# Twenty-two instead of sixteen expert tiles scored ahead of the expert loop of a two-block transformer kernel

## What is computed

```python
def peer(x, w_q, sub_keys, u_tab, v_tab):
    q = (xt @ w_q).reshape(T, PEER_HEADS, 2, PEER_HALF)
    s = jnp.einsum('thpd,hpkd->thpk', q, sub_keys)
    s_top, i_top = lax.top_k(s, PEER_TOPK)
    cand = s_top[:, :, 0, :, None] + s_top[:, :, 1, None, :]
    best, pos = lax.top_k(cand, PEER_TOPK)
    gate = jax.nn.softmax(best, axis=-1)
    act = gelu(einsum('td,thkd->thk', xt, u_tab[eid]))
    return einsum('thk,thkd->td', gate * act, v_tab[eid])
```

## Time and profile before

| | |
|---|---|
| Median of three runs | 3553.58 us (3553.43 to 3553.96) |
| The profiled execution, its own time | 3553.21 us |
| Its span | 3551.4 us |
| Mean granted TensorE clock | 0.966 of full speed |
| Busy share: PE, PEld, DVE, ACT, POOL | 94%, 82%, 66%, 42%, 11% |
| First L696 of the three layers | at 256.01, 1369.77 and 2744.74 us |
| Moved by transfers | 511.71 MB, 144 GB/s on average |

### The profile page before, as it was taken

The page is one execution under the profiler, slowest core; times in us unless marked ns, Lnnn a source line. Parts: engine busy times, 40 slices in busy tenths (PEclk is TensorE's granted clock), DMA queues, the critical chain, the costliest instruction groups (busy, mean ns, idle before and its releaser), DMA issues. The chain is left out here.

```text
span 3551.4 us, 58703 instructions
## 1 busy us (share of the span) xinstructions
PE 3327.6 (94%) x20974; PEld 2901.9 (82%) x20974; DVE 2329.5 (66%) x4413; ACT 1485.1 (42%) x2257; POOL 387.8 (11%) x412
## 2 busy tenths in 40 slices
PE   7889999999987798999999996989889999999998
PEld 5788899999986587899999996578478889999996
DVE  4697666666656588766666665555459766666665
ACT  3336444444444325544444433333333644444444
POOL 0156000000000047300000000000015700000000
PEclk9899999999998699999999998999999999999999
DMA  5420555555543131355555545100232055555553
GB/s 208 152 74 28 188 184 186 189 189 185 183 164 150 52 139 48 105 193 184 187 189 189 185 164 185 63 1 1 95 147 79 22 187 189 189 183 185 187 189 145
DMA packets 127130, 511.71 MB, mean 144 GB/s; under 512 B 14624, under 2 KB 15520, under 8 KB 119712
## 3 DMA queue, kind: packets, MB, share of 16 engines
q1 hardware_dynamic: 127008, 510.09, 40.4%
HBM read 508.99 MB, written 1.05 MB: 144 GB/s over the span
## 5 line engine op out<-in xcount | busy, mean ns | idle before, releaser
L610 PE MATMUL ps<-xh,uhigh 128*128 128x256 f32 x3072 | 870.4, 283 | 0.0
L612 PE MATMUL ps<-xh,ulow 128*128 128x256 f32 x3072 | 869.3, 283 | 0.0
L611 PE MATMUL ps<-xl,uhigh 128*128 128x256 f32 x3072 | 869.2, 283 | 0.0
L610 PEld LDWEIGHTS ps<-xh,uhigh 128*128 128x128 f32 x3072 | 588.3, 191 | 14.6 <-issue 1.4
L611 PEld LDWEIGHTS ps<-xl,uhigh 128*128 128x128 f32 x3072 | 588.3, 192 | 14.3 <-issue 1.4
L612 PEld LDWEIGHTS ps<-xh,ulow 128*128 128x128 f32 x3072 | 588.3, 191 | 0.0
L760 ACT CAST uhigh<-stream 128x1024 fp32r<-128x1024 f32 x336 | 352.8, 1050 | 442.4 <-DMA stream<-in_u 442.4
L992 DVE TENSOR_TENSOR ulow<-stream,uhigh 128x1024 fp32r<-128x1024 f32 x330 | 404.4, 1225 | 194.5 <-ACT uhigh L760 194.4
L997 DVE TENSOR_TENSOR stream<-stream,big 128x256 f32<-128x256 f32 x336 | 217.9, 649 | 411.2 <-ACT stream L822 411.1
L628 PE MATMUL ps<-vhigh,chigh 128*128 128x512 f32 x1536 | 479.8, 394 | 1.5 <-DVE vlow L1008 1.5
L628 PE MATMUL ps<-vlow,chigh 128*128 128x512 f32 x1536 | 476.0, 391 | 0.0
(11 more groups left out here) (498 smaller groups left out, 4383.6 us busy)
## 6 DMA issues: line engine op xcount, KB each, us to landing
stream<-in_u SPq DMA_DIRECT2D x369, 512.0 KB, 4.2
stream<-in_v SPq DMA_DIRECT2D x369, 512.0 KB, 3.5
big<-in_wq SPq DMA_DIRECT2D x24, 1152.0 KB, 7.1
stream<-in_ab_w_in SPq DMA_DIRECT2D x4, 2048.0 KB, 10.9
stream<-in_c_w_qf SPq DMA_DIRECT2D x16, 512.0 KB, 3.5
stream<-in_c_w_ig SPq DMA_DIRECT2D x4, 2048.0 KB, 9.0
big<-in_w_gates SPq DMA_DIRECT2D x4, 2048.0 KB, 8.3
spare<-in_u SPq DMA_DIRECT2D x15, 512.0 KB, 3.6
```

Of the source, the lines that this page charges most:

```text
L610: pe.matmul(out, high[:, cols], c.xh[:, k, :], start=k == 0, stop=False)
L611: pe.matmul(out, high[:, cols], c.xl[:, k, :], start=False, stop=False)
L612: ins = pe.matmul(out, low[:, cols], c.xh[:, k, :], start=False, stop=k == KD - 1)
```

## The change

One constant is raised:

```diff
-HELD = 16
+HELD = 22
 SLOTS = 4
 WCOLS = 2 * KD * P + 2 * P
 GROUP = 2
```

## The result

The changed kernel takes 3559.02 us in the median (3553.26 to 3563.12, 22 runs) against 3553.85 us (3551.72 to 3556.03, 22 runs) before: a ratio of 1.0016, interval 1.0010 to 1.0022. That is 5.2 us slower. The profiled execution took 3557.37 us, its span 3555.2.

The account below looks back on a forecast made before the run. PE, 94% busy, bounds the kernel except in an idle stretch ended by a chain from POOL's last low part. 3 x (0.2 + 1.6) = 5.3 us on 3553.2 gives 3558.5, median 0.4 higher: 3559 us, range 3550 to 3566.

Parts of the forecast that it names:

- PE's work is moved and not saved: Per layer: loop 33.7 us less, held outputs 16.6 and held scores 17.3 more, so PE's work grows by 0.2 us.
- The stretch moves with POOL's last low part: PE's idle stretch before the first L696 is pushed on by 17.28 us per layer, not filled.
- the chain: Transfer, ACT, POOL, DVE: 15.25 us from the last held low part's end to the first L696, moving with the held tiles.
- The turns: POOL's low parts alternate with DVE's L925 and L869, 3.33 us a turn; the chain starts 1.6 us late per layer.
- Gate matrix and loads at nothing: Wider gate_held and ACT's shorter copies: 0, bounds -1.8 and +1.4 us; v loads slowing the u tile: 0, at most 0.9 per layer.
- the first (the idle time is filled): Rival: PE's three waits of about 5.41 us before the distances are all covered; 3538 us; chance 0.05.
- The second: Rival: the stretch shifts but DVE's four instructions fit POOL's gaps or the delay is made good; 3554 us; chance 0.18.
- the fourth: Rival: L945 gets its turn between POOL's two low parts, 2.3 us back per layer; 3552 us; chance 0.08.
- The third: Rival: DVE and POOL instructions exclude each other at full length, 3.62 us a turn; 3562.5 us; chance 0.21.
- the rule of the Trainium skill: The shared pair of ports is held for the full instruction and the other side fully blocks; by it, 3562.5 us.
- the signs named in the prediction: Among them: first L696 about 19 us later, low parts over 3 us, L940 done some 10 us before the exponential.

Follow-up runs that it names:

- act22: Changed kernel, but ACT makes the high parts of the loop's first two tiles behind the exponential, not before the last two gelus: 3552.44 us.
- all22: Changed kernel with the three edits of psum22, late22 and act22 together: 3538.38 us, again 3538.80; ratios to the kernel before 0.9957, 0.9958.
- psum22: Changed kernel, but in the last round DVE reads ranks and indices for L925 and L869 from PSUM: 3552.48 us, ratio to the kernel before 0.9996.
- late22: Changed kernel, but POOL makes the low parts of the loop's first two tiles behind its last one-hot columns of the gate matrix: 3549.71 us.
- vwait22: Changed kernel, but SP issues the first v loads only when both u loads ahead have landed: 3558.45 us, ratio to the kernel before 1.0015.

## Why the prediction was right

The time came out at 3559.0, the number forecast, and the steps can be held against the rows:

- *PE's work is moved and not saved.* Held outputs +16.6 a layer as forecast, loop -33.4 on average (33.7 forecast), 0.3 short by the second layer's idle time.
- *The stretch moves with POOL's last low part.* Forecast for the first L696 of the first layer: 256.01 + 17.28 + 1.6 = 274.9; measured 275.57 less the 0.81 by which the layer began late, 274.8. act22 and all22 show that the chain is real, since cutting it at the exponential brings the L696 forward though L940 stays.
- *The turns.* Forecast 3.33 us each; the two L869 took 6.56 and two low parts 6.74, so 3.3 to 3.4. The last held low part ended at 260.37 - 0.81 = 259.6 as forecast, and counted from the start of its layer it ended 18.8, 19.0 and 18.5 us later than number 15 had, where 18.9 was forecast. psum22 takes just this away and with it the loss.
- *Gate matrix and loads at nothing.* The gate matrix took 0.2 us less on average, within the bounds, but one term behind it was mis-sized. `gate_held` takes 329 ns in the median and not 273 + 22, since the 0.91 ns per element came from two different operations (the row stands below). 64 x 56 ns would be 3.6 us a layer, outside the bound of 1.4. It did not count: DVE waits for PE there, as the prediction says, and with the clock taken off nothing is left of it. The u tile took 4.8, 5.0 and 4.8 us from its issue to ACT's cast, against 4.8, 5.7 and 4.9 before, so in the second layer the loads gave 0.7 us back.

```profile
L957 DVE TENSOR_TENSOR big<-big,ps x192: 314/329/344, 280.4 to 2850.2; 128x88 f32<-128x88 f32 x192
```

The sum by layers is 4.5 us where 5.3 was forecast: the first L696 moved by 18.45 us on average and not by 18.9 (-1.3 us over three layers), the gate matrix took less (-0.6), and the loop gave less back (+1.0). That the median hit to the tenth is luck: these misses offset each other in part, the rest of the program varies by more than they do, and the executions spread over 10 us.

Of the rivals, the first (the idle time is filled) is refuted by the 11.76 us; it also priced PE's wait at 5.41 us in all three layers, and in the second it was 3.79. The second is refuted by low parts of 3.2 to 3.4 us; the fourth by L945, 2.59 us in each layer. The third had the mechanism but not the size: a turn took 3.34 us and not the 3.62 of both reported lengths. Of the rule of the Trainium skill, "SBUF — State Buffer", section "Who interferes with whom", the exclusion held. The same section says that a DVE instruction with at most one SBUF input, outside the 2-port perf modes, does not contend with GpSimd. The trace of psum22 agrees for L925 and L869, 1.22 us each beside POOL. One SBUF input alone is no safeguard, though: L940, a cast with a single one, takes 0.29 us alone (second layer) and 2.35 beside low part 21; no row names its mode.

Among the signs named in the prediction, one was off: L940 was to be done some 10 us before the exponential; it ended at 260.5, 8.6 us before, as it was itself held by low part 21.

## What to carry to other kernels

Before work is put into an idle stretch, follow the chain that ends the stretch back to where it begins: if it begins at the work itself (here the last low part releases a transfer, and the transfer stands in ACT's order before the softmax), more work pushes the stretch on. First take the chain off, by putting what the next stage waits for ahead of what only a later one needs, and then fill: here the reordering took 10.4 us off the three layers with 16 tiles, and six more tiles then took off 2 to 3 us more (one profile each), where alone they cost 4.5. And look at which engine pairs will newly run side by side; DVE's instructions with two SBUF inputs and POOL's took turns, and one operand in PSUM ended that. An order that frees one such instruction can put the next beside POOL's work, as act22 did.

## What the runs showed of the hardware

- Two instructions that exclude each other took 3.34 us a turn (start to start of POOL's low parts), less than the 3.62 of their reported lengths; so 0.2 to 0.3 us of the reported lengths seem to lie outside the exclusion.
- DVE's cast L940, with one SBUF input, took 0.29 us while POOL was idle and 1.3 to 2.4 us when issued beside a low part.
- After an idle stretch PE's granted clock was at 0.50 for another 3.5 to 9.8 us of work in the layers of before, of the changed kernel and of act22, and the gate matrix was longer by about half of that.
- Two identical u loads behind the same event landed after 4.6 to 5.2 us in the layers of before, of the changed kernel, psum22 and vwait22 that I read (5.7 in one), and after 6.5 to 6.9 in two of late22. In the second layer of all four kernels with 16 tiles it was 5.7 to 6.2. No run here says why.
- Executions of the changed kernel spread more (3553.3 to 3563.1) than those of the kernel before (3551.7 to 3556.0).
